# A two-block network on one core: x turned unscaled ahead of two stages, a Fourier transform by token parity, and sigmoids moved inside the last substitution

## The reference, cut to what matters

```python
def _rmsnorm(x, g):
    y = x * lax.rsqrt(jnp.mean(x * x, axis=-1, keepdims=True) + EPS)
    return y * g

def _odd_layer(x, norm_g, w_in, ...):
    z = _rmsnorm(x, norm_g) @ w_in
    cq, ckv, ik, iw, gate = _split_cols(z, [512, 256, 64, 16, 2048])
    cq = _rmsnorm(cq, q_norm)
    ...
    ckv = _rmsnorm(ckv, kv_norm)
    ik = _layernorm(ik, ik_g, ik_b)
    iw = iw * (IDX_HEADS ** -0.5 * IDX_DIM ** -0.5)
    ...
    return (o * jax.nn.silu(gate)) @ w_out          # then x = x + this

def fourier_branch(f, w_lin):                       # 8 groups of 128 columns
    fr = jnp.real(jnp.fft.fft2(fg, axes=(1, 3), norm="ortho"))   # over tokens and columns
    return fr @ w_lin

# second block
q, k, v, z, f, scal, gates = jnp.split(rms_norm(x, g_mix) @ w_in, SPLIT_POINTS, axis=-1)
gate_a, gate_f = jnp.split(jax.nn.sigmoid(gates), 2, axis=-1)
x = x + (gate_a * y_a + gate_f * y_f) @ w_o
h = rms_norm(x, g_mlp)
x = x + jnp.square(jax.nn.relu(h @ w_mlp_up)) @ w_mlp_down
```

## Time and profile before

| | us |
|---|---|
| median of 3 runs | 2259.07 (2258.32 to 2259.59) |
| the profiled execution | 2259.39 |
| its span, first to last instruction | 2257.6 |
| PE busy | 2192.3 (97%) |
| POOL, ACT, DVE busy | 1717.2, 1036.1, 1026.1 |
| PE waiting for the scaled x of the norms | 19.9 in four waits |
| mean granted clock of PE | 0.991 |

### The profile page before, as it was taken

The page is one execution under the profiler, slowest core; times in us unless marked ns, Lnnn a source line. Parts: engine busy times, 40 slices in busy tenths (PEclk is TensorE's granted clock), DMA queues, the critical chain, the costliest instruction groups (busy, mean ns, idle before and its releaser), DMA issues.

```text
span 2257.6 us, 34155 instructions
## 1 busy us (share of the span) xinstructions
PE 2192.3 (97%) x12554; PEld 1882.7 (83%) x12554; DVE 1026.1 (45%) x1762; ACT 1036.1 (46%) x1442; POOL 1717.2 (76%) x721
## 2 busy tenths in 40 slices
PE   7999999999999999999999999999999999999997
PEld 6888888878888778888888888887888888888886
DVE  3981242024853141657474834305813822831841
ACT  5434455454556554535354545444333333333343
POOL 6888868877667865657575757897888888888885
PEclk9999999999999999999999999999999999999999
DMA  7666545646455754545454545665666666666664
GB/s 216 189 188 191 181 140 172 193 129 180 140 150 166 228 152 124 146 116 160 116 153 121 159 121 169 204 201 157 190 191 193 187 195 189 192 189 194 187 194 140
DMA packets 321438, 384.10 MB, mean 170 GB/s; under 512 B 14654, under 2 KB 255141, under 8 KB 321061
## 3 DMA queue, kind: packets, MB, share of 16 engines
q1 hardware_dynamic: 317237, 376.75, 55.8%
q10 hardware_dynamic: 4080, 5.64, 0.8%
HBM read 380.24 MB, written 2.10 MB: 169 GB/s over the span
## 4 chain that ended last, share of the span: by engine, by line
PE 92%; DVE 2%; ACT 2%; issue 2%; POOL 1%; DMA 1%; ACTq 0%; POOLq 0%; DVEq 0%
PE lin_ps L1942 36%; PE lin_ps L1945 18%; PE lin_ps L1982 9%; PE lin_ps L1983 9%; PE lin_ps L1981 9%; POOL w_lo L582 1%; PE ps L1914 1%; PE ps L2312 1%; ACT w_hi L610 1%; DMA raw<-in_odd_w_out 0%; PE ps L2244 0%; PE lin_ps L2106 0%; PE lin_ps L2107 0%; PE lin_ps L2108 0%; PE lin_ps L2167 0%
## 5 line engine op out<-in xcount | busy, mean ns | idle before, releaser
L582 POOL TENSOR_TENSOR w_lo<-raw,w_hi 128x1024 fp32r<-128x1024 f32 x716 | 1716.9, 2405 | 521.1 <-ACT w_hi L610 424.2
L1942 PE MATMUL lin_ps<-a,w_hi 128*128 128x512 f32 x3200 | 1022.1, 401 | 0.9 <-POOL w_lo L582 0.8
L610 ACT ACTIVATE w_hi<-raw 128x1024 fp32r<-128x1024 f32 x456 | 479.2, 1059 | 570.1 <-PE lin_ps L1945 359.6
L1945 PEld LDWEIGHTS lin_ps<-a,w_lo 128*128 128x128 f32 x3200 | 602.5, 188 | 142.4
L1945 PE MATMUL lin_ps<-a,w_lo 128*128 128x256 f32 x3200 | 630.4, 278 | 0.0
L1942 PEld LDWEIGHTS lin_ps<-a,w_hi 128*128 128x128 f32 x3200 | 492.3, 190 | 8.6 <-issue 5.2
L621 ACT ACTIVATE w_hi<-raw 128x1024 fp32r<-128x1024 f32 x228 | 242.1, 1062 | 384.8 <-PE lin_ps L1945 225.6
L1981 PE MATMUL lin_ps<-w_hi,b 128*128 128x512 f32 x704 | 274.7, 390 | 1.9 <-POOL w_lo L582 1.8
L1982 PE MATMUL lin_ps<-w_lo,b 128*128 128x512 f32 x704 | 274.0, 389 | 0.0
L1983 PE MATMUL lin_ps<-w_hi,b 128*128 128x512 f32 x704 | 273.9, 389 | 0.0
L1981 PEld LDWEIGHTS lin_ps<-w_hi,b 128*128 128x128 f32 x704 | 132.2, 188 | 30.6 <-POOL w_lo L582 3.3
(11 more groups left out here) (379 smaller groups left out, 2094.0 us busy)
## 6 DMA issues: line engine op xcount, KB each, us to landing
raw<-in_w_in SPq DMA_DIRECT2D x144, 512.0 KB, 3.7
raw<-in_w_mlp_up SPq DMA_DIRECT2D x128, 512.0 KB, 3.8
raw<-in_w_mlp_down SPq DMA_DIRECT2D x128, 512.0 KB, 3.7
raw<-in_even_w_in SPq DMA_DIRECT2D x112, 512.0 KB, 3.7
raw<-in_odd_w_in SPq DMA_DIRECT2D x40, 512.0 KB, 3.7
raw<-in_even_w_out SPq DMA_DIRECT2D x32, 512.0 KB, 3.9
raw<-in_odd_w_out SPq DMA_DIRECT2D x32, 512.0 KB, 4.6
raw<-in_w_o SPq DMA_DIRECT2D x32, 512.0 KB, 4.3
```

The source lines that it names most:

```text
L582: nc.gpsimd.tensor_tensor(w_lo[:, slot], raw[:, slot], w_hi[:, slot].bitcast(F32), ALU.subtract).then_inc(lo_done, 1)
L610: nc.scalar.activation(w_hi[:, slot], raw[:, slot], ACT.Copy).then_inc(hi_done, 1)
L1942: nc.tensor.matmul(lin_ps[:, 2 * parity + m, :], hi[:, k, m * P:(m + 1) * P], src[:, kk].rearrange("p s n -> p (s n)"), start=(q == 0 and ...
L1945: last = nc.tensor.matmul(lin_ps[:, 2 * parity + m, 0:T], lo[:, k, m * P:(m + 1) * P], src[:, kk, 0, :], start=False, stop=(q == n - 1 and ...
```

## The change

Three things are changed.

1. Rounds 1 and 3 of the norms. x is no longer scaled by the reciprocal root before it is turned. `turn_x` turns x itself, block n - 1 at unit 6 of block n of the projection before (even_w_out or w_o_2), and the last block before chunk 4 of the next product. The halves of these blocks are made in the projection too (`upper` in `projection`, `lower` in `to_x`), into the chunks of `a` (r = 1, shifted by 8) or `b` (r = 3) that are free then. The missing factor is applied later. In the odd layer: in the squares and normings of cq and kv, in iw and ik, and for the gates by a row of reciprocals over tokens (`by_row`, made by two products on PE and a copy on ACT after cq), which DVE multiplies into each gate group in place. In the MLP: by its square in the sums into x. The MLP's hidden values go to `a` instead of `b`.
2. The Fourier transform over tokens is split by parity. The first transform takes the even tokens, then the odd ones, as its stationary side; the second makes two halves of 128 output tokens, ACT copies one out, DVE adds and subtracts. The table comes in five transfers instead of one.
3. The sigmoids of the mix gates. For six of the eight rows of each group they stand between high halves inside the last pair, the rest behind the first round of the mix.

```diff
+LATE = {1: "even_w_out", 3: "w_o_2"}
+SCALED = {0: 0, 2: 1}
+TURN_AT = 6
...
# ACT: inside projection(name, r, n)
+                def upper(n):
+                    for j in range(4):
+                        c = 4 * n + j
+                        act.wait_ge(nm_pe.sem, nm_pe.at(f"{c // 2}", r))
+                        g = ROWS[NORMS[r]] + c
+                        nc.scalar.activation(late(r, c)[:, 0, :], ps[:, 2 * (n % 2) + j // 2, (j % 2) * T:(j % 2 + 1) * T], ACT.Copy,
+                                             scale=vec[:, g:g + 1]).then_inc(nm_hi.sem, 1)
...
-                for j in range(4, 35):
+                last_turn = 4 if r == 3 else 5
+                for j in range(4, 40):
                     hi(u0 + j, (u0 + j) % SLOTS)
                     if j in (12, 20, 28):
                         added(name, (j - 12) // 8)
                         squares(r, (j - 12) // 8)
-                added(name, NB - 1)
-                squares(r, NB - 1)
+                    if j in (8 + TURN_AT + 3, 16 + TURN_AT + 3, 24 + TURN_AT + 3):
+                        upper((j - TURN_AT - 3) // 8 - 1)
+                    if j == 35:
+                        added(name, NB - 1)
+                        squares(r, NB - 1)
+                    if j == 32 + last_turn:
+                        upper(NB - 1)
                 roots_of(r)
...
# ACT: odd layer
-            norm(1, ODD)
...
             his_to(8, 10)
+            act.wait_ge(gt_pe.sem, gt_pe.at("rows"))
+            nc.scalar.activation(by_row[:], ps[:, 3, 0:T], ACT.Copy).then_inc(gt_act.sem, 1)
             act.wait_ge(unit_used, OU["cq"] + 8)
...
# ACT: tables
-                    act.dma_start(z[:, Z_DFT:Z_DFT + 5, :], t["c_dft"]).then_inc(table_in, 16)
+                    act.dma_start(z[:, Z_DFT, :], t["c_dft"][:, 0, :]).then_inc(table_in, 16)
+
+                    for q in range(TT):
+                        for k in range(TT):
+                            act.dma_start(z[64 * k:64 * k + 64, Z_DFT + 1:Z_DFT + 3, q * P:(q + 1) * P],
+                                          t["c_dft"][q:P:2, 1 + k:4 + k:2, 0:P]).then_inc(table_in, 16)
...
# ACT: Fourier groups
-                nc.scalar.activation(b[:, 8 + g, 0, :], ps[:, 3, 0:T], ACT.Copy).then_inc(fo_act.sem, 1)
+                nc.scalar.activation(z[:, Z_DFT + 3, 0:P], ps[:, 3, P:2 * P], ACT.Copy).then_inc(fo_act.sem, 1)
+                act.wait_ge(fo_dve.sem, fo_dve.at("diff", g))
+                nc.scalar.activation(b[:, 8 + g, 0, :], ps[:, 3, T:2 * T], ACT.Copy).then_inc(fo_act.sem, 1)
...
# ACT: last pair and mix
-                fill(16, 17, 18, 19, 20, 21)
+                for n in range(16, 22):
+                    fill(n)
+                    if p == PAIRS - 1 and n < 20:
+
+                        act.wait_ge(group_free, FILL_G + 24)
+                        gate = z[:, 8 * (n - 16):8 * (n - 16) + 6, :]
+                        nc.scalar.activation(gate, gate, ACT.Sigmoid).then_inc(mx_act.sem, 1)
...
-            act.wait_ge(group_free, GROUP0["gates"] + 16)
-            for n in range(4):
-                gate = z[:, 8 * n:8 * n + 8, :]
-                nc.scalar.activation(gate, gate, ACT.Sigmoid).then_inc(mx_act.sem, 1)
...
+            mixed(0)
+
+            act.wait_ge(group_free, GROUP0["gates"] + 16)
+            gate = z[:, 0:32, :].rearrange("p (n r) c -> p n (r c)", n=4)[:, :, 6 * T:8 * T]
+            nc.scalar.activation(gate, gate, ACT.Sigmoid).then_inc(mx_act.sem, 1)
+            with act.Fori(1, 8) as i:
+                mixed(i)
...
# DVE: to_x
+                        by = own_scale if own_scale is not None else scale
+                        nc.vector.scalar_tensor_tensor(out=xs, in0=xs if own_scale is None else acc, scalar=by[:, q:q + 1] if by is not None else 1.0,
+                                                       in1=acc if own_scale is None else xs, op0=ALU.mult,
                                                        op1=ALU.add).then_inc(group_free if q else x_half, 1)
+                    if r is not None:
+                        lower(n)
...
# DVE: gate_out
             def gate_out(n):
                 dve.wait_ge(unit_used, OU[f"gate{n}"] + 4)
+                dve.wait_ge(gt_act.sem, gt_act.at("rows"))
+                bank = 2 * (OG[f"gate{n}"] % 2)
+                both = lin_ps[:, bank:bank + 2, :].rearrange("p m (s n) -> p m s n", s=2)
+                nc.vector.tensor_tensor(both, both, by_row[:].unsqueeze(1).unsqueeze(1).broadcast_to([P, 2, 2, T]), ALU.mult).then_inc(gt_dve.sem, 1)
+                dve.wait_ge(gt_dve.sem, gt_dve.at(f"g{n}"))
                 group_out(f"gate{n}", 0, z[:, Z_OGATE + 2 * n:Z_OGATE + 2 * n + 2, :])
...
# DVE: small operations ahead of the turn of kv
-                nc.vector.tensor_scalar(cqn[q], lin_ps[:, q, :], stat[:, 44 + q:45 + q], None, ALU.mult).then_inc(own, 1)
+                nc.vector.tensor_scalar(cqn[q], lin_ps[:, q, :], stat[:, 44 + q:45 + q], recip[:, q:q + 1], ALU.mult, ALU.mult).then_inc(own, 1)
...
+            nc.vector.tensor_tensor(stat[:, 50:52], recip, recip, ALU.mult).then_inc(own, 1)
...
+            nc.vector.tensor_tensor(stat[:, 42:44], stat[:, 42:44], recip, ALU.mult).then_inc(own, 1)
...
# DVE: Fourier groups
+                dve.wait_ge(fo_act.sem, fo_act.at("odd", g))
+                for n, op in ((0, ALU.add), (1, ALU.subtract)):
+                    nc.vector.tensor_tensor(ps[:, 3, T + n * P:T + (n + 1) * P], ps[:, 3, 0:P], z[:, Z_DFT + 3, 0:P], op).then_inc(fo_dve.sem, 1)
                 dve.wait_ge(fo_act.sem, fo_act.at("hi", g))
...
# PE
+            def turn_x(r, n):
+
+                name = LATE[r]
+                pe.wait_ge(x_half, NB * PLAIN.index(name) + n + 1)
+                pe.wait_ge(group_free, OUTS[name][1] + n + 1)
+                for half in range(2):
+                    if n >= 2:
+                        pe.wait_ge(nm_lo.sem, nm_lo.at(f"{4 * (n - 2) + 2 * half + 1}", r))
+                    for j in (2 * half, 2 * half + 1):
+                        for q in range(TT):
+                            m = nc.tensor.transpose(ps[:, 2 * (n % 2) + half, (j % 2) * T + q * P:(j % 2) * T + (q + 1) * P],
+                                                    x[:, q, n * BLK + j * P:n * BLK + (j + 1) * P], ident[:])
+                    m.then_inc(nm_pe.sem, 1)
+
+            def turned_in(r):
+                def wait(c):
+                    if c == 4:
+                        turn_x(r, NB - 1)
+                    pe.wait_ge(nm_lo.sem, nm_lo.at(f"{c}", r))
+                return wait
...
                 for n in range(NB):
                     for j in range(done if n == 0 else 0, 8):
+                        if r is not None and n and j == TURN_AT:
+                            turn_x(r, n - 1)
                         outer_unit(name, src, n, j, waits)
...
+                if name == "cq":
+
+                    pe.wait_ge(nm_rs.sem, nm_rs.at("rn1", 1))
+                    for q in range(TT):
+                        m = nc.tensor.matmul(ps[:, 3, q * P:(q + 1) * P], recip[:, q:q + 1].broadcast_to([P, P]), ident[:], start=True, stop=True)
+                    m.then_inc(gt_pe.sem, 1)
...
-                    m = nc.tensor.matmul(ps[:, 2, q * T:(q + 1) * T], z[:, Z_F + g, q * P:(q + 1) * P], z[:, 40, :], start=True, stop=True)
+                    m = nc.tensor.matmul(ps[:, 2, q * T:(q + 1) * T], z[:, Z_F + g, q:T:2], z[:, Z_DFT, :], start=True, stop=True)
...
-                        m = nc.tensor.matmul(ps[:, 3, 0:T], z[:, 48 + q, s * P:(s + 1) * P], z[:, 41 + 2 * s + q, :],
-                                             start=(q == 0 and s == 0), stop=(q == 1 and s == 1))
+                        m = nc.tensor.matmul(ps[:, 3, q * P:(q + 1) * P], z[:, 48 + q, s * P:(s + 1) * P], z[:, Z_DFT + 1 + s, q * P:(q + 1) * P],
+                                             start=(s == 0), stop=(s == 1))
...
-                linear(UNIT0["mlp"] + 64 * ph, GROUP0["mlp"] + 12 * ph, 8, 4, a, waits=normed(3) if ph == 0 else None)
-                projected(f"mlp{ph}", of_b, hid_ready)
+                linear(UNIT0["mlp"] + 64 * ph, GROUP0["mlp"] + 12 * ph, 8, 4, b, waits=turned_in(3) if ph == 0 else None)
+                projected(f"mlp{ph}", of_a, hid_ready)
```

More of the change, by code:

```diff
@@ L286, in build @@
         mg_sq = steps("mg_sq", [f"s{n}{q}" for n in range(NB) for q in range(TT)] + ["root1"])
+        sq_dve = steps("sq_dve", ["r2"])
+        gt_pe = steps("gt_pe", ["rows"])
+        gt_act = steps("gt_act", ["rows"])
+        gt_dve = steps("gt_dve", [f"g{n}" for n in range(8)])
         preloaded = sem("preloaded")
@@ L324, in build @@
         sc_dve = steps("sc_dve", ["wlo", "feat", "a0", "a1", "neg", "abs", "pos", "sp", "nea", "g0", "g1", "gc", "rem", "ne"])
-        fo_act = steps("fo_act", ["ab", "hi"])
+        fo_act = steps("fo_act", ["ab", "odd", "hi"])
         fo_pe = steps("fo_pe", ["ab", "o"])
-        fo_dve = steps("fo_dve", ["lo"])
+        fo_dve = steps("fo_dve", ["sum", "diff", "lo"])
```

(24 more changed lines are left out.)

89 lines of the change are left out of this document (52 added, 37 removed).

## The result

| | before | after |
|---|---|---|
| median | 2258.70 (2256.51 to 2259.59, 4 runs) | 2243.55 (2242.29 to 2243.86, 4 runs) |
| the profiled execution | 2259.39 | 2242.29 |
| its span | 2257.6 | 2240.5 |
| mean granted clock | 0.991 | 0.994 |

The ratio is 0.9933, 95% interval 0.9916 to 0.9951; five more runs of the changed kernel in a later session gave 2243.77 and 0.9928 (0.9914 to 0.9941). The changed kernel is faster, clear of noise, and the time lies inside the forecast's range of 2236 to 2249.5 us. The two profiled executions differ by 17.10 us.

What follows compares the result with a forecast made beforehand. PE, busy 97% of the span, was taken to bound the kernel. 23.8 us gained less 7.7 given back made 16.1 net: 2259.4 to 2243.3 us, with a range of 2236 to 2249.5.

Steps and rivals of the forecast that it cites:

- Norms r=1 and r=3: PE's idle time and turns before cq and the MLP mostly go: gains of 6.86 and 6.24 us.
- The cover: At both norms: fourth block's sum and chunk 12's low halves ready before PE needs them; 1.2 us spare in r=3.
- Fourier: Second transform, eight groups, 0.84 us less each: 6.7 gained; strided loads taken as 0, upper bound 5.2.
- Mix: Before the mix: PE's idle 2.16 us and the halved clock's 1.58 go, 3.7 gained.
- The cover of unit 8: In the mix: POOL ends unit 8's low half 1.0 us before PE wants it.
- Gates: Odd layer, DVE's multiplies cost PE 3.05 (gates 1-3), 1.27 (gate 4), 2.4 us (gates 5-7, after slack).
- Turn of kv: Odd layer: four more small operations before it, covered by two gate units (5.6 us): nothing, 0.7 without cover.
- Clock and tables: Odd layer: possible clock drop of 1.6 us, put at half, 0.8 lost; smaller c_dft table: 0.3 gained.
- Gates hidden (2236): Rival, odd layer: DVE's idle time hides the gate multiplies, only 0.5 us given back, 2236; chance 0.10.
- Gates or strided loads dearer: Rival: 5.2 us for Fourier loads, or one to three more odd-layer clock drops, 2245 to 2248.5; chance 0.18.
- Waits moved (2253): Rival: PE waits for the fourth block or chunk 12, both norms keep their 5.0 us, 2253; chance 0.05.
- Slower (2283): Rival: each of eight turns inside the projections waits 5.0 us, 40 us against 16.1 gained, 2283; chance 0.03.

Runs made afterwards that it cites:

- unit-0 run: The changed kernel with the three inner turns of round 3 at unit 0 of the next block instead of unit 6: 2247.71 us, ratio 0.9951.
- Fourier run: The kernel before with only the Fourier change (parity split, table in five transfers): 2251.01 us, ratio 0.9964.

## Why the prediction was right, and where it was not

- **Norms r=1 and r=3**: right in kind and size (6.44 and 6.22 against 6.66 and 6.24). The cover held: neither the fourth block nor chunk 12 made PE wait, and the clock stayed at 1.00. The unit-0 run shows this for the inner turns of r=3: there the sum's time was covered, it was not zero.
- **Fourier**: 6.62 against 6.7. The strided load cost nothing (0.86 per piece), as I took it without a row to show it; the upper bound of 5.2 was never near. The rule of the Trainium skill (SBUF — State Buffer, section Door 1: The DMA port swizzle), that float32 may stride as long as a second element of each 16-byte line is used, agrees with the traces: 189 ns at a stride of one, 195 at two, 325 at four.
- **Mix**: 3.99 against 3.7; the idle time was worth 2.33 start to start and not the 2.16 of the bracket, and the halved clock 1.66, a little over the 1.58. This second part was luck: in the Fourier run the same wait left the clock at 1.00, and there the move would have been worth 2.3 only (an estimate). The cover of unit 8 was 0.5 to 0.8 us where I had 1.0. No drain of 1.38 us follows the table load here: the late sigmoid starts 0.01 us after it, and PE did not wait for unit 8.
- **Gates**: 6.68 in all against 6.72, by the same three mechanisms. Gates 1 to 3 cost 0.45 less; of 5 to 7 the last costs its full 1.28 where I took the slack of 0.47 off, since in that round ACT's high halves and POOL's low halves stand behind the scaling and PE waits for them. The run without the multiply confirms the whole.
- **Turn of kv**: the step that failed. "A chain that PE covers with two gate units, 5.6 us: nothing" was wrong; PE waited 0.44 and the stretch grew by 0.73, the price that the prediction put on a lost cover (0.7). I counted four small operations by their usual 0.15 to 0.2 us. One of them, the square of the reciprocals (L1466), took 2.04: both its inputs lie in SBUF, POOL had begun a subtraction at 508.31, and L1466 ended 0.02 us after that subtraction did. In the kernel before, the scaled kv is ready 4.4 us after kv's last product, 2.5 before PE asks for it; now it takes 7.4, and 1.9 of the 3.0 more are L1466. Without these 1.9 it would be ready 1.3 us before PE asks (an estimate; no run took L1466 alone out of the chain). The timelines of DVE and POOL in the changed kernel:

```profile
508.31 2.41 POOL L597 TENSOR_TENSOR w_lo<-raw,w_hi 128x1024 fp32r<-128x1024 f32 x1
...
508.70 2.04 DVE L1466 TENSOR_TENSOR stat<-nst 128x2 f32<-128x2 f32 x1
...
513.20 0.16 DVE L1473 TENSOR_TENSOR stat<-stat,nst 128x2 f32<-128x2 f32 x1
```

The same form takes 0.16 us at 513.20 with POOL idle. The profile of the kernel before could have told. In its selection a product of 128 columns in SBUF (L1472) takes 2.40 us:

```profile
586.84 2.40 DVE L1472 TENSOR_TENSOR dmask<-z,causal 128x128 bf16<-128x128 f32 x1
```

- **Clock and tables**: the drop that I gave half a chance did not come (0.8), and odd_w_out gave 1.6 instead of 0.3, most of which is no effect of the change. These two are 2.1 us in favour; the turn of kv (0.7) and small misses took 1.1 back, and 17.1 stands beside the forecast's 16.1. The medians differ by 15.2. So the 0.3 us of the heading is luck in part: single stages miss by up to 1.3.
- **Rivals**: the traces exclude each. Gates hidden (2236): they cost 6.7. Gates or strided loads dearer: 6.68 where 6.72 was put, 0.86 per piece, no clock drop in the odd layer. Waits moved (2253): no PE wait at the turns of x. Slower (2283): the same.

## What to carry to other kernels

A wait at a norm goes if the matrix is turned before it is scaled, but the scale comes back as work elsewhere: look where it lands. Here the landing place (a product of 1024 columns in PSUM, ahead of a bank's release and of the scores) ate the whole gain of one of the two norms, and the same product on 512 columns, behind the release and where DVE and POOL both idle, gave it back: 6.7 us for moving the multiply. Before a small DVE operation is costed at nothing, see whether both inputs are in SBUF and what POOL does then.

## What the runs showed of the hardware

- DVE operations with both inputs in SBUF and POOL's subtraction shut each other out: 2.04 for two columns and 2.88 us for 512 when POOL was at it, 0.16 and 0.67 when it idled; POOL's four low halves 10.96 instead of 9.44 when DVE came first. It is no rare case: the subtraction that makes the low half of each MLP hidden group (L1964, 512 columns, both inputs in SBUF) takes 2.9 us all 32 times, each time ending 0.55 us after a low half of POOL, and 2.9 in the kernel before too. PE is not held up by it there. The eight multiplies of the changed kernel that read PSUM (L1423) all took 1.20 to 1.23. The Trainium skill (SBUF — State Buffer, section Who interferes with whom) has this as an exclusive lock held for a whole instruction; the trace agrees. I had not applied it. Moving L1466 out of that chain was not tried. The row of L1964 (busy us, mean ns):

```profile
L1964 DVE TENSOR_TENSOR a<-scr,a 128x512 f32 x32 | 92.6, 2893 | 4.7 <-DVE a L1962 0.6
```

- Idle times of 1.5 to 1.7 us in a full stream left the clock at 1.00 three times. An idle time of 2.16 before the mix halved it in the kernel before, one of 2.17 at the same place did not in the Fourier run. So the length of a wait alone does not tell whether the clock falls; what else decides it is open.
- The clock falls in two or three of the four pairs, in other ones from kernel to kernel with the same work there, at some 1.4 us each, and the opening is 1.0 to 1.5 us longer in some profiles. Single profiles of one kernel differ by that: 2240.5 and 2242.8 for the changed one.
